# Three edits in the recurrence stage of a hybrid encoder layer: middle level products over the later query halves only, the state's last two steps behind the fifth masked copy, the convolution's squares product two groups later

## The reference, cut to what matters

```python
def _conformer_conv(u, dw_w, dw_b, ln_g, ln_b):
    ...
    mu = jnp.mean(hf, axis=-1, keepdims=True)
    var = jnp.mean(jnp.square(hf - mu), axis=-1, keepdims=True)
    hf = (hf - mu) * lax.rsqrt(var + EPS) * ln_g.astype(jnp.float32) + ln_b.astype(jnp.float32)
    ...
def _hgrn2_chunk_step(S, inp):
    q, k, v, g = inp
    b = jnp.cumsum(g, axis=2)
    causal = jnp.tril(jnp.ones((CHUNK, CHUNK), bool))[:, :, None]
    decay = jnp.exp(jnp.where(causal, b[:, :, :, None, :] - b[:, :, None, :, :], -jnp.inf))
    A = jnp.einsum('bhtd,bhsd,bhtsd->bhts', q, k, decay)
    o = jnp.einsum('bhtd,bhde->bhte', q * jnp.exp(b), S) + jnp.einsum('bhts,bhse->bhte', A, v)
    ...
```

## Time and profile before

| | |
|---|---|
| median of 3 runs | 493.64 us (493.01 to 495.23) |
| the profiled execution's own time | 493.04 us |
| its span in the profile | 491.2 us |
| TensorE busy | 466.5 us, 95% |
| TensorE weight loads busy | 310.6 us, 63% |
| VectorE busy | 283.5 us, 58% |
| ScalarE busy | 149.5 us, 30% |
| GpSimd busy | 37.4 us, 8% |
| mean granted clock of TensorE | 0.988 of full |

### The profile page before, as it was taken

The page is one execution under the profiler, slowest core; times in us unless marked ns, Lnnn a source line. Parts: engine busy times, 40 slices in busy tenths (PEclk is TensorE's granted clock), DMA queues, the critical chain, the costliest instruction groups (busy, mean ns, idle before and its releaser), DMA issues.

```text
span 491.2 us, 10555 instructions
## 1 busy us (share of the span) xinstructions
PE 466.5 (95%) x4292; PEld 310.6 (63%) x4292; DVE 283.5 (58%) x699; ACT 149.5 (30%) x366; POOL 37.4 (8%) x45
## 2 busy tenths in 40 slices
PE   8999999999999999999999999989999899796795
PEld 6888898888786444555656655655665555355342
DVE  5898999999878975338584332333442222231256
ACT  4350237530157423330153221221222111121134
POOL 0000000100001000000012021101202111000000
PEclk9999999999999999999999999999999999987999
DMA  8990000000009999539798999999999999999994
GB/s 304 352 383 21 0 1 1 3 1 1 3 3 309 415 426 424 236 107 415 259 377 345 417 354 415 422 424 424 420 424 416 424 422 425 421 426 424 421 389 192
DMA packets 28593, 143.00 MB, mean 291 GB/s; under 512 B 4373, under 2 KB 10677, under 8 KB 19840
## 3 DMA queue, kind: packets, MB, share of 16 engines
q1 hardware_dynamic: 22864, 131.03, 66.0%
q0 software_dynamic: 5248, 10.85, 6.1%
q10 hardware_dynamic: 432, 0.44, 0.3%
HBM read 133.21 MB, written 16.78 MB: 305 GB/s over the span
## 4 chain that ended last, share of the span: by engine, by line
PE 67%; DMA 20%; DVE 6%; SPq 5%; issue 1%; ACT 1%; DVEq 0%; ACTq 0%
PE bank_pair L1583 13%; PE bank_pair L1923 10%; PE bank_pair L1784 9%; DMA area_g<-in_w_exp 8%; DMA area_w<-in_w_exp 7%; PE bank_pair L1946 5%; PE bank_pair L1593 4%; PE bank_pair L1931 4%; DMA area_w<-in_w_out 4%; PE bank_pair L1533 3%; PE bank_pair L1721 3%; SPq L524 3%; DVE area_m L938 2%; PE bank_pair L1916 2%; PE bank_pair L1954 2%; PE bank_pair L1548 1%
## 5 line engine op out<-in xcount | busy, mean ns | idle before, releaser
L1784 PE MATMUL bank_pair<-area_w,area_m 128*128 128x512 f32 x128 | 57.2, 596 | 0.3 <-DMA area_w<-in_w_out 0.3
L938 DVE SCALAR_TENSOR_TENSOR area_m<-area_g,cols,area_m 128x512 f32<-128x512 f32 x60 | 41.3, 742 | 0.0
L1923 PE MATMUL bank_pair<-area_w,area_m 128*64 128x256 f32 x320 | 38.5, 383 | 1.6 <-DMA area_w<-in_w_exp 1.6
L1784 PEld LDWEIGHTS bank_pair<-area_w,area_m 128*128 128x128 f32 x128 | 23.5, 190 | 26.0 <-issue 25.5
L1923 PEld LDWEIGHTS bank_pair<-area_w,area_m 128*64 128x64 f32 x320 | 21.9, 137 | 16.5 <-issue 6.5
L1923 PE MATMUL bank_pair<-area_g,area_m 128*64 128x256 f32 x256 | 31.1, 385 | 1.2 <-DMA area_g<-in_w_exp 1.2
L2159 DVE COPY cst<-bank_pair 128x128 f32<-128x128 f32 (+1 forms) x36 | 9.5, 263 | 36.6 <-PE bank_pair L1937 28.0
L2177 DVE COPY area_m<-bank_pair 64x512 f32<-64x512 f32 x20 | 13.9, 694 | 22.9 <-PE bank_pair L1946 22.9
L1923 PEld LDWEIGHTS bank_pair<-area_g,area_m 128*64 128x64 f32 x256 | 17.7, 136 | 12.5 <-issue 4.3
L2166 DVE TENSOR_TENSOR cst<-cst,bank_pair 128x128 f32<-128x128 f32 x22 | 6.4, 289 | 32.6 <-ACT cst L2080 32.6
L1931 PE MATMUL bank_pair<-area_w,area_m 128*32 128x128 f32 x512 | 21.1, 320 | 2.8 <-DMA area_w<-in_w_exp 2.8
(11 more groups left out here) (444 smaller groups left out, 865.9 us busy)
## 6 DMA issues: line engine op xcount, KB each, us to landing
area_g<-in_w_exp SPq DMA_DIRECT2D x14, 2048.0 KB, 32.3
area_w<-in_w_exp SPq DMA_DIRECT2D x13, 2048.0 KB, 22.9
area_w<-in_w_exp SPq DMA_DIRECT2D x16, 1024.0 KB, 21.6
area_g<-in_w_exp SPq DMA_DIRECT2D x14, 1024.0 KB, 32.0
area_x<-in_w_exp SPq DMA_DIRECT2D x4, 2048.0 KB, 25.0
area_w<-in_w_in SPq DMA_DIRECT2D x6, 1024.0 KB, 12.4
area_w<-in_w_out SPq DMA_DIRECT2D x2, 2048.0 KB, 15.3
expert_out<-area_g SPq DMA_DIRECT2D x2, 2048.0 KB, 22.6
```

The costliest lines, as they stand in the source:

```text
L938: ins = V.scalar_tensor_tensor(out=mixT[:, i, :], in0=src, scalar=w, in1=mixT[:, i, :], op0=ALU.mult, op1=ALU.add)
L1784: ins = T.matmul(bank[PROJECT_BANK[i]][:, :], mixT[:, k, j * P:(j + 1) * P], w_out_sb[:, n, k, :], start=(k == 0), stop=(k == KT - 1))
L1923: ins = T.matmul(out_b[h * BC:(h + 1) * BC, 0:2 * P], x[:, k, :], w_gate_up[slot][:, :, k, h * P:(h + 1) * P], start=(k == 0), stop=(k == ...
```

## The change

Three edits. First, the products of the middle levels (16 to 1, groups 2 to 11) move only the later query halves, 32 columns picked with a stride pattern, and write only those columns of the bank; their stationary operand stays 64 keys wide. Second, of VectorE's seven state steps the first five stay in front (STATES_AHEAD = 6), and the last two go behind mask 4. Third, SQUARES_AT goes from 4 to 6: TensorE's squares product from behind group 4 to behind group 6, and with it VectorE's sum of squares from behind mask 3 to behind mask 5.

```diff
         SCORES_AT = 8
         MEANS_AT = 1
-        SQUARES_AT = 4
+        STATES_AHEAD = 6
+        STATES_AT = 4
+        SQUARES_AT = 6
         NORM_AT = 8
...
             step(V.tensor_copy(state[:, 0, :, :], bank[0][:, 0:P].rearrange("p (i e) -> p i e", i=2)))
-            for c in range(1, NC_):
+            def state_step(c):
+
                 u = bank[c // 4][:, (c % 4) * P:(c % 4) * P + P].rearrange("p (i e) -> p i e", i=2)
                 for i in range(2):
...
                     else:
                         ins.then_inc(state_done, 1)
+
+            for c in range(1, STATES_AHEAD):
+                state_step(c)
...
                 if n == SQUARES_AT - 1:
                     dve.wait_ge(conv_factor, 1)
                     V.tensor_tensor(osq[:, 0, :], osq[:, 0, :], osq[:, 1, :], ALU.add).then_inc(conv_factor, 1)
+                if n == STATES_AT:
+                    for c in range(STATES_AHEAD, NC_):
+                        state_step(c)
                 if n in ADD_AT:
                     add_part("q1", C12 + ADD_AT.index(n))
...
+            def later(cols_of, h):
+
+                return cols_of.rearrange("p (r t) -> p r t", t=2 * h)[:, :, h:]
+
             nl = len(LEVELS)
...
                         else:
-                            kk = qq = lev[l][s, ti, t]
-                        ins = T.matmul(bank[2 + n % 2][s, t], kk, qq, start=True, stop=True)
+                            kk = lev[l][s, ti, t]
+                            qq = later(kk, LEVELS[l])
+                        made_in = bank[2 + n % 2][s, t]
+                        if 0 < l < nl:
+                            made_in = later(made_in, LEVELS[l])
+                        ins = T.matmul(made_in, kk, qq, start=True, stop=True)
```

## The result

The changed kernel took 500.01 us (median of 22 executions, 493.55 to 501.47) against 493.91 us for the kernel before (22 executions, 493.01 to 495.23). The medians stand as 1.012 to 1. The ratio of the fast executions is 1.0056 with a 95% interval of 1.0032 to 1.008; those more than 1.5% above the fastest are left out of it, so it understates what follows. The forecast was 494.2.

The account below looks back on a forecast made before the run. TensorE's chain between 124 and 148 us was taken to release the transfer-bound last third. No product saving plus 0.6 us of waiting gave 493.64 profiled, 494.2 us median; stated range 491.7 to 495.2.

Parts of the forecast that it names:

- two rules of the Trainium skill: For the middle products: spacing by moving columns alone (saves 4.3 us), or load time by columns of weights (saves 0).
- the formula: Rule giving an isolated matmul's spacing by its moving columns alone; for the middle products it promised 4.3 us.
- The walk: Step-by-step timing from group 4 to the squares product: start at about 135.45, after TensorE stands still 0.9 us.
- Gain in front: VectorE reaching the masks earlier with two state steps moved: 0.05 us taken before mask 2.
- the sum: TensorE's waits before the scores added up: 0.7 us today, 1.26 after, so +0.6 us.
- the factor of 1: TensorE time won or lost between 124 and 148 us moves the end one for one; 0 as lower end.
- the release: First output's end lets SyncE issue the output projection's weights; third-phase loads stand behind it; forecast about 0.6 us later.
- The rival: Clock falls because TensorE counts as less busy with half the columns moving: likely 497.6 us, chance 0.05.
- its price: Cost of the clock falling to 1.2 GHz: likely 3.4 us more, on top of the forecast.

Follow-up runs that it names:

- e11: Edit 1 in the old order, stationary operand of groups 2 to 11 also cut to 32 keys (a pace measurement only): 492.28 us, ratio 0.995.
- e2: Changed kernel with products 64 columns wide again, so edits 2 and 3 alone: 494.67 us, ratio 1.0022, none of 12 long.
- e4: The changed kernel measured again, nothing altered: 500.91 us, nine of 12 executions long.
- e1: Changed kernel with state steps and squares product back in the old order, so edit 1 alone: 494.49 us, ratio 1.0009, none of 12 long.
- e3: Changed kernel with all seven state steps in front again, so edits 1 and 3: 494.04 us, ratio 1.0018, one of 12 long.
- e9: Changed kernel plus a 512-column product filling the wait before the squares product: 494.68 us, ratio 0.9999, none of 12 long.
- e8: Changed kernel with the last two state steps behind mask 5 and the sum of squares (STATES_AT 5, not 4): 493.75 us, ratio 0.9994.
- e12: Changed kernel with only groups 2 to 6 narrow, run a second time: 495.96 us, ratio 1.0019; profile at 496.41 us.
- e5: Changed kernel with only groups 2 to 6 narrow, first run: 495.47 us, ratio 1.0028; profile at 493.53 us.
- e10: Changed kernel with four state steps behind mask 4, not two (STATES_AHEAD 4): 502.95 us, ratio 1.0155, all six executions long.

## Why the prediction was wrong, point by point

**Right: edit 1 saves nothing.** Records with 32 columns moving and 64-wide weights are 29 ns apart, as L1859 said, and e11 shows the other side. The prediction set two rules of the Trainium skill against each other, both from "TensorE: Matmul & The Clock Gate". From the section "Back-to-back issue gap" it took the formula; that section's table gives every width from 1 to 64 columns one spacing, about 60 cycles or 25 ns, by which edit 1 would save nothing either. But groups 12 and 13 run at 15.8 ns a record, below the table's figure, and the measurement decides.

**Right: edits 2 and 3 cost a wait.** The walk gave a squares product at 135.45 behind the state steps and mask 5; it started at 135.29 in the profile (135.19 with wide products), with that order ahead of it. The wait is 0.68 us where I had 0.9. Gain in front: mask 2 starts at 130.58 in place of 130.65 (group 0 itself 0.03 earlier), and I had taken 0.05. In time the two edits alone come to a ratio of 1.0022, about 1.1 us with an interval of 0.6 to 1.6 where the sum said 0.6; in the stage itself e2's profile shows 0.55. The ten short executions have a median of 494.3 against 494.2 predicted.

**Right within a microsecond or two: the factor of 1.** 6.5 us at the release are 6.7 at the end. That the two agree so well is in part luck: in e4's profile 6.8 us at the release (154.72) are 8.0 at the end, and over all profiles the end moved from 0.1 us less to 1.7 us more than the release, against the kernel before.

**Wrong: the weighing of the clock.** The step that failed is the sentence "here TensorE stands still only 0.9 us at a time, and the clock stayed full through groups 12 and 13 and through L1859; but those are short". I held the wait and the narrow products against the clock one at a time, each with its own rows, and each passed. They are neighbours: five narrow groups run from 129.27 up to the wait. That "TensorE stands still only 0.9 us at a time" was true (0.68), and it was no argument against the fall. e1, e3 and e2 show that each alone is nearly harmless (1 long execution of 36), and e4, e9 and e8 that the two together are not. The rival had 0.05 where it happened in 21 of 34 executions.

**Wrong: its price.** I put the fall at 3.4 us of extra time, from no row of the trace. The low stretch was 13.6 us long in the profile, from 135 to 148.6, and groups 7 to 11 behind the wait were narrow. From one start to the next, after against before: squares product 2.01 for 1.05, groups 7 and 8 3.55 for 2.01, scores 1.26 for 0.69, groups 9 and 10 3.56 for 2.01, last part of q1 3.38 for 1.92. That is 6.1 us in all; with about 0.5 of waiting it is the 6.5. The rows of before for the last three, behind those of the earlier trace rows:

```profile
138.56 2.08 PE L1721 MATMUL bank_pair<-area_w 64*64 64x64 f32 x64
140.57 1.99 PE L1583 MATMUL bank_pair<-area_x,area_w 128*128 128x256 f32 x8
142.49 2.48 PE L1721 MATMUL bank_pair<-area_w 64*64 64x64 f32 x96
```

With wide groups behind (e12) the low stretch was 3.4 us long, ended by 140 and cost 1.6 us.

**What stays open.** Which executions of the same kernel fall, and which don't, I can't say. Both profiles of the changed kernel are long ones; e5 and e12, one kernel, have the same work and the same wait ahead of the squares product, and the clock fell in one profile only. Whether it is the number of moving columns that matters or the stepped way in which the narrow products read and write them is not separated, since every narrow product of groups 2 to 11 has both. What brings the clock back is not shown either: in e10 it stayed low through products in which it rose in the changed kernel. Nor is it shown why e11 holds its clock with narrow products and longer waits, nor why an execution of the kernel before took 499.69 us once.

No version beats the kernel before by more than a measurement tells. The order of e8 is the one to take if the narrow products are wanted.

## What to carry to other kernels

A wait on TensorE that cost 0.6 us by itself cost ten times as much here where the products ahead of it moved few columns; ask of each new wait what runs on either side, and look for a second sort of execution in the single times before trusting a median. Narrowing the moving operand saved nothing while the stationary one stayed wide; look for a row that has the one without the other. When two engines pass work back and forth at fixed places, put an operation that nobody waits for behind the one that somebody does: here that is one constant, 5 for 4.

## What the runs showed of the hardware that I had not expected

The granted clock has two levels in these traces, 1.2 and 2.4 GHz, and it fell during a standstill of TensorE of only 0.68 us, or just behind it (e12), with 5.3 us of narrow products ahead (129.27 to 134.61). TensorE's busy time alone doesn't tell this case from the harmless one: from 130 to 136 us it is busy 1.87, 2.00 and 1.32 of 2 us here, and 1.90, 2.00 and 1.35 with wide products (e2), where no execution was long. The Trainium skill, "TensorE: Matmul & The Clock Gate", section "Why this matters for your kernels", warns of idle gaps between bursts that are several times as long as this one. The gap was 0.68 us in two long profiles, and the measurement decides.

At the low level records with 64-wide weights and 32 columns moving are (3.63 - 0.29) / 63 = 53 ns apart in place of 29 (0.29 us is one record's own length there), and the squares product, with 512 columns moving, holds TensorE 2.01 us in place of 1.05. So the pace that the weights set goes down with the clock as the columns' does.
